# Modulation vectors of a two-block transformer kernel: column sums with TensorE replaced by row dot products on VectorE, with a new order of the opening and buffers moved to multiples of 512 bytes

## The reference: what is computed

```python
mod = silu(c) @ w_ada + b_ada            # 1024 -> 6 * 1024
sh1, sc1, g1, sh2, sc2, g2 = split(mod, 6)
h = rms_norm(x, norm_mix_g) * (1.0 + sc1) + sh1
proj = h @ w_in + b_in                   # 1024 -> 9224: GLU, q/k, v, o, gates, merge
a = glu; a = causal_depthwise_conv(a); a = silu(layer_norm(a)); y_conv = a @ w_conv_pw
y_mlstm = ...                            # chunkwise mLSTM over q, k, v and the gates
x = x + g1 * ((g_conv * y_conv + g_mlstm * y_mlstm) @ w_out)
h = rms_norm(x, norm_ffn_g) * (1.0 + sc2) + sh2
x = x + g2 * ((silu(h @ w_gate) * (h @ w_up)) @ w_down)
x = rms_norm(x, final_norm_g)
```

## Time and profile before

| | |
|---|---|
| median of 3 runs | 1706.56 us (1702.82 to 1707.67) |
| the profiled execution | 1704.14 us, of which the span in the trace is 1702.2 us |
| busy in the span | PE 1617.2 us, weight load 1312.4, DVE 1022.8, ACT 623.3, POOL 114.1 |
| mean granted TensorE clock | 0.977 of full speed |
| moved by DMA | 172.87 MB, 102 GB/s in the mean |

### The profile page before, as it was taken

The page is one execution under the profiler, slowest core; times in us unless marked ns, Lnnn a source line. Parts: engine busy times, 40 slices in busy tenths (PEclk is TensorE's granted clock), DMA queues, the critical chain, the costliest instruction groups (busy, mean ns, idle before and its releaser), DMA issues.

```text
span 1702.2 us, 18384 instructions
## 1 busy us (share of the span) xinstructions
PE 1617.2 (95%) x7176; PEld 1312.4 (77%) x7176; DVE 1022.8 (60%) x1527; ACT 623.3 (37%) x881; POOL 114.1 (7%) x94
## 2 busy tenths in 40 slices
PE   5999898999999899999999998999989999999988
PEld 4887776778778788888888886778867888888867
DVE  6699888889668644333464447766566444442255
ACT  3221465654442342222233233546453222222223
POOL 0000000000000000000011001000142111100010
PEclk9999988999899899999999999999999999999999
DMA  9133221222446334233332321211332333333332
GB/s 357 50 99 104 70 74 63 62 75 87 148 173 210 100 122 141 96 96 92 92 108 82 116 78 61 82 44 38 98 101 87 95 93 98 99 93 96 96 112 74
DMA packets 48191, 172.87 MB, mean 102 GB/s; under 512 B 5349, under 2 KB 5477, under 8 KB 47849
## 3 DMA queue, kind: packets, MB, share of 16 engines
q1 hardware_dynamic: 48104, 171.70, 31.6%
HBM read 167.48 MB, written 4.19 MB: 101 GB/s over the span
## 4 chain that ended last, share of the span: by engine, by line
PE 83%; DVE 11%; ACT 3%; issue 2%; DMA 0%; POOL 0%; SPq 0%; DVEq 0%; POOLq 0%; ACTq 0%
PE bank L1329 24%; PE bank L1330 24%; PE bank L1337 23%; DVE tmp L1874 1%; PE bank L1349 1%; DVE spl L1723 1%; PE bank L1351 1%; PE bank L1350 1%; DVE convout L1808 1%; PE bank L1432 1%; PE bank L1415 1%; PE bank L1445 1%; DVE XT L2211 1%; PE bank L1365 1%; ACT tmp L1498 1%
## 5 line engine op out<-in xcount | busy, mean ns | idle before, releaser
L1329 PE MATMUL bank<-HH,sph 128*128 128x512 f32 x1480 | 600.7, 406 | 28.9 <-DVE spl L1723 11.3
L1330 PE MATMUL bank<-HH,spl 128*128 128x512 f32 x1480 | 588.3, 397 | 0.0
L1723 DVE TENSOR_TENSOR spl<-raw,sph 128x1024 fp32r<-128x1024 f32 (+1 forms) x261 | 330.9, 1269 | 316.9 <-ACT sph L1490 316.5
L1337 PE MATMUL bank<-HL,sph 128*128 128x512 f32 x1480 | 385.9, 395 | 0.9 <-DVE HL L2215 0.9
L1329 PEld LDWEIGHTS bank<-HH,sph 128*128 128x128 f32 x1480 | 284.5, 192 | 100.6 <-issue 26.9
L1490 ACT ACTIVATE sph<-raw 128x1024 fp32r<-128x1024 f32 (+1 forms) x261 | 269.6, 1034 | 216.0 <-PE bank L1337 166.1
L1330 PEld LDWEIGHTS bank<-HH,spl 128*128 128x128 f32 x1480 | 285.0, 193 | 59.9 <-issue 1.4
L1337 PEld LDWEIGHTS bank<-HL,sph 128*128 128x128 f32 x1480 | 280.1, 190 | 63.2 <-DVE HL L2215 2.2
L1808 DVE SCALAR_TENSOR_TENSOR convout<-convin,vecs,convout 128x512 f32<-128x512 f32 x240 | 166.7, 745 | 0.0
L1329 PE MATMUL bank<-midh,sph 128*128 128x512 f32 x352 | 138.7, 394 | 0.0
L1330 PE MATMUL bank<-midh,spl 128*128 128x512 f32 x352 | 138.7, 394 | 0.0
(11 more groups left out here) (294 smaller groups left out, 1567.7 us busy)
## 6 DMA issues: line engine op xcount, KB each, us to landing
raw<-in_w_in SPq DMA_DIRECT2D x73, 512.0 KB, 3.6
raw<-in_w_up SPq DMA_DIRECT2D x66, 512.0 KB, 3.6
more<-in_w_ada SPq DMA_DIRECT2D x32, 512.0 KB, 4.5
raw<-in_w_down SPq DMA_DIRECT2D x32, 512.0 KB, 3.5
raw<-in_w_gate SPq DMA_DIRECT2D x22, 512.0 KB, 3.6
ada<-in_w_ada SPq DMA_DIRECT2D x16, 512.0 KB, 14.6
raw<-in_w_down SPq DMA_DIRECT2D x16, 384.0 KB, 3.1
raw<-in_w_v SPq DMA_DIRECT2D x8, 512.0 KB, 3.6
```

Source lines behind the costliest of these rows:

```text
L1329: e.matmul(P_[b][:], sph(n)[:, q], hi[:, k, :], start=k == 0, stop=False)
L1330: e.matmul(P_[b][:], spl(n)[:, q], hi[:, k, :], start=False, stop=False)
L1337: m = e.matmul(P_[b][:], sph(n)[:, q], low[:, k, :], start=False, stop=last and k == kb - 1)
L1723: e.tensor_tensor(spl(n), raw(n), sph(n).bitcast(F32), ALU.subtract).then_inc(*up("s_w_low", ("wl", n)))
```

## The change

Four parts.

1. `w_ada` is laid out transposed: one load of 512 KB now holds 128 outputs on the partitions and all 1024 inputs along them. A tile of `mod` is then one dot product on VectorE of the load with `silu(c)`, which stands as a row of 1024 on every partition (`crow`, a broadcast load, and a Silu of 128x1024 on ScalarE). Bias and sum are in the same instruction, and the products overwrite the load. `mod_sum`, `mod_far`, `mod_cols`, `mod_tiles` and `ada_columns` go, and with them all one-column matmuls of the modulation; `modacc` goes.
2. The opening's order: the loads begin with `x`, then the row of `c`, then `vecs` and `consts`; the Silu stands behind the squares of the first norm; the first four dot products stand ahead of the norm's root; from there each pair's dot products stand directly behind the low parts of the pair before, at k = 0 and 2 instead of at odd k.
3. The row of `c` is loaded and put through Silu a second time, after fence "gc", since its first place is used by others in between.
4. Buffers move: `base` from 16512 to 16896, `B` rounded up to a multiple of 512 bytes, `ah` and `al` too. So all high and low activations and the three weight slots start at multiples of 512 bytes. `sph_first`, `sph_second` and `spl_first` do not.

The first `csil` below is SyncE's, the second ScalarE's.

```diff
-    mod_a, mod_b, mod_c = misc.take(), misc.take(), misc.take()
...
-    csil, gmix = keepc(8), keepc(8)
-    add("csil", csil)
+    gmix = keepc(8)
     ss = SumSq("x0")
     for i in range(8):
         ss.add(("XT", i), [("x", 0, i)])
+    add("csil", 0)
+    add("mod_dots", 0)
     b0 = rows_of(ss, D)
...
     def mod_pair(p):
-        add("mod_far", p, mod_a[0], [("mod_half", p - 1)] if p else mod_a[1])
-        add("mod_cols", p, accs[p][0], mod_c[0], [("mod", p - 1)] if p else mod_c[1])
-        tmp.give(accs[p][0], ("mod_cols", p))
-        add("mod_tiles", p, mod_a[0], mod_c[0])
...
+        if p:
+            add("mod_dots", p)
+        low[p] = [tmp.take() for _ in range(2)]
         for z in range(2):
-            add("norm", "n1", 2 * p + z, *js[z], b0, [])
+            add("norm", "n1", 2 * p + z, *low[p][z], b0, [])
...
-    mod_sum(0, 0, 6)
     split()
     split()
     mod_pair(0)
-    mod_sum(1, 0, 3)
+    mod_low(0)
+    mod_pair(1)

     def mod_feed(k):
-        p = k // 2
-        if k % 2 == 0 and p < 3:
-            mod_sum(p + 1, 3, 6)
-            if p < 2:
-                mod_sum(p + 2, 0, 3)
-        if k % 2 and p < 3:
-            mod_pair(p + 1)
+        if k % 2 == 0 and k < 6:
+            mod_low(k // 2 + 1)
+            if k < 4:
+                mod_pair(k // 2 + 2)
+            else:
+                add("zero_pads")
...
     side.append(layer_norm())
+    add("csil", 1)
     add("ada_more", 0)
     add("ada_more", 1)
...
-        base = 16512
+        base = 16896
...
+        o += -(base + o) % 512
         B = o
+        CROW[0] = place("crow0", B + 13056, [128, 1024])
...
-        AH = place("ah", B + 33728, [128, 8, S], F32R)
-        AL = place("al", B + 33728 + 16384, [128, 8, S], F32R)
+        AH = place("ah", B + 33792, [128, 8, S], F32R)
+        AL = place("al", B + 33792 + 16384, [128, 8, S], F32R)
...
+            def csil(n):
+                if n:
+                    w.wait_ge(*fenced("gc"))
+                    e.dma_start(CROW[1][:], A["c_row"].broadcast_to([128, 1024])).then_inc(
+                        *up("d_c1", ("c_all", 1), by=16))
...
+            def csil(n):
+                w.wait_ge(at("c_all", n))
+                e.activation(CROW[n][:], CROW[n][:], ACT.Silu).then_inc(*up("s_ada_a", ("csil", n)))
...
+            def mod_dot(buf, n, et, label):
+                e.tensor_tensor_reduce(buf, buf, CROW[n][:], 1.0, vec("b_ada", et), ALU.mult, ALU.add,
+                                       MOD[:, et:et + 1]).then_inc(*up("s_ada", label))
+
+            def mod_dots(p):
+                w.wait_ge(at("csil", 0), at("vecs"))
+                for z in range(4):
+                    w.wait_ge(at("ada_w", p, z))
+                    mod_dot(ADA[4 * p + z][:], 0, 2 * p + z % 2 + 8 * (z // 2), ("mod", p, z))
...
             def ada(u):
-                k, s = u % 8, KEEP[:, u % 8:u % 8 + 1]
-                w.wait_ge(at("more", u))
-                if k == 0:
...
-                    ins = e.tensor_scalar(ACC[:], MORE[more(u)][:], s, None, ALU.mult)
-                else:
-                    w.wait_ge(at("ada", u - 1))
-                    ins = e.scalar_tensor_tensor(ACC[:], MORE[more(u)][:], s, ACC[:], ALU.mult, ALU.add)
-                ins.then_inc(*up("s_ada", ("ada", u)))
+                w.wait_ge(at("more", u), at("csil", 1))
+                mod_dot(MORE[more(u)][:], 1, 16 + u, ("ada", u))
```

More of the change, by code:

```diff
@@ L372, in plan, with mod_low @@
         ss.add(("XT", i), [("x", 0, i)])
+    add("csil", 0)
+    add("mod_dots", 0)
     b0 = rows_of(ss, D)
[L374 to L380, removed]
-    def mod_pair(p):
-        add("mod_far", p, mod_a[0], [("mod_half", p - 1)] if p else mod_a[1])
-        add("mod_cols", p, accs[p][0], mod_c[0], [("mod", p - 1)] if p else mod_c[1])
-        tmp.give(accs[p][0], ("mod_cols", p))
-        add("mod_tiles", p, mod_a[0], mod_c[0])
-        js = [tmp.take() for _ in range(2)]
+    low = {}
+    def mod_pair(p):
+        if p:
+            add("mod_dots", p)
+        low[p] = [tmp.take() for _ in range(2)]
         for z in range(2):
-            add("norm", "n1", 2 * p + z, *js[z], b0, [])
+            add("norm", "n1", 2 * p + z, *low[p][z], b0, [])
+    def mod_low(p):
         for z in range(2):
-            add("normlo", "n1", 2 * p + z, js[z][0])
-            tmp.give(js[z][0], ("hi", "n1", 2 * p + z), ("lo", "n1", 2 * p + z))
-    mod_sum(0, 0, 6)
+            add("normlo", "n1", 2 * p + z, low[p][z][0])
+            tmp.give(low[p][z][0], ("hi", "n1", 2 * p + z), ("lo", "n1", 2 * p + z))
     split()
@@ L1310, in end @@
                 w.wait_ge(at("out", 7))
-            run({"begin": begin, "load": load, "ada_load": ada_load, "ada_more": ada_more, "v_begin": v_begin, "rot_load": rot_load,
+            run({"begin": begin, "load": load, "ada_load": ada_load, "csil": csil, "ada_more": ada_more, "v_begin": v_begin, "rot_load": rot_load,
                  "w2_begin": w2_begin, "rd_load": rd_load, "p_load": p_load, "e_spill": e_spill,
@@ L1743, in spread @@
                         *up("s_scale", ("diag", name, t)))
[L1745 to L1770 removed]
+            def mod_dot(buf, n, et, label):
[6 more added lines that the diff above has]
+                    mod_dot(ADA[4 * p + z][:], 0, 2 * p + z % 2 + 8 * (z // 2), ("mod", p, z))
+                g8 = GMIX + 2 * p
+                w.wait_ge(at("mod", p, 3))
                 e.scalar_tensor_tensor(KEEP[:, g8:g8 + 2], MOD[:, 8 + 2 * p:10 + 2 * p], 1.0,
@@ L2321, in x2_lo @@
                         *up("s_cut_p", ("lo", "x2", i)))
-            run({"begin": begin, "split": split, "sum": total, "v_begin": v_begin, "decay_begin": decay_begin,
+            run({"begin": begin, "zero_pads": zero_pads, "split": split, "sum": total, "v_begin": v_begin, "decay_begin": decay_begin,
                  "normlo": normlo, "up": up_, "rope_full": rope_full, "mix_ret": mix_ret, "x2_lo": x2_lo,
@@ L2363, in layout @@
     o["pos"] = np.ascontiguousarray(x["positions_2"].reshape(1, S))
-    ada = x["w_ada"][0].reshape(8, 128, 6, 1024)
-    first = ada[:, :, 0:2].reshape(4, 2, 128, 2, 4, 256).transpose(4, 0, 2, 1, 3, 5)
-    o["w_ada1"] = np.ascontiguousarray(first).reshape(4, 4, 128, 2, 512)
-    o["w_ada2"] = np.ascontiguousarray(ada[:, :, 2:].transpose(2, 0, 1, 3)).reshape(32, 128, 1024)
+    ada = np.ascontiguousarray(x["w_ada"][0].T).reshape(48, 128, 1024)
+    pairs = [[2 * p + z % 2 + 8 * (z // 2) for z in range(4)] for p in range(4)]
+    o["w_ada1"] = np.ascontiguousarray(ada[np.array(pairs)])
+    o["w_ada2"] = np.ascontiguousarray(ada[16:])
+    o["c_row"] = np.ascontiguousarray(x["c"][0].reshape(1, D))
     o["w_in"] = _tiles(np.concatenate([win[:, 0:4096], win[:, 5120:6144], win[:, 6152:8200]], axis=1))
```

110 lines of the change are left out of this document (27 added, 83 removed).

## The result

| | before | after |
| --- | --- | --- |
| median of 4 runs each | 1704.69 us (1702.62 to 1707.67) | 1686.45 us (1686.18 to 1687.87) |
| profiled execution: time, span | 1704.14, 1702.2 us | 1687.87, 1686.1 us |

The ratio is 0.9893, with a 95% interval from 0.9874 to 0.9913: 18.2 us less. The forecast was 1686.6.

The account below looks back on a forecast made before the run. TensorE, busy 95% of the span, was taken as the bound, waiting for VectorE in the opening and behind fence "gc". Terms -6.8 - 6.8 + 2.6 - 8.9 = -19.9 us gave 1684.2, plus 2.4 for the median 1686.6; range 1677 to 1698.

Parts of the forecast that it names:

- Dot product at 1.3 us: Modulation on VectorE: one dot product over two SBUF tiles of 1024 costs 1.3 us, bounded by 1.15 and 1.5.
- half rate: Rival, chance 0.08: dot products run at half rate, 2.35 us each; time 1706 us, no change.
- The opening, 6.8 us saved: Opening: without column sums and the clock's fall, the last product of k = 8 starts at 61.5, not 68.33.
- So the early start is worth nothing: Opening: first product 1.3 us earlier, but the stall moves behind the third unit; k = 1 starts 0.4 us later.
- Second row of `c`, 2.6 us lost: Behind fence "gc": the second load and Silu delay the layer norm's chain, lengthening TensorE's wait; bounds 0 to 5 us.
- Column sums, 6.8 us saved: Later modulation: four column sums of 1.7 us each leave TensorE's queue; VectorE has room for 32 dot products.
- Addresses, 8.9 us saved: Matmuls: 1366 products each 6.5 ns faster once activation and weight start at the same place within 512 bytes.
- 352 bytes past: Placements before the change: the prediction put the starts of `midh` and `midl` 352 bytes past a multiple of 512.
- nothing: Rival, chance 0.10: the addresses give nothing, products stay at 233 ns; time 1695.5 us.
- frees the stream: Rival, chance 0.06: a multiple of 512 frees the stream altogether, 213 ns a product; time about 1603 us.
- collides: Rival, chance 0.05: two streams starting at multiples of 512 collide, 4728 `HH` products 6.5 ns longer; 1726 us.
- Sum: Whole kernel: the four terms total -19.9 us against the profiled 1704.14; with 2.4 for the median, 1686.6 us.

Follow-up runs that it names:

- splits first: Changed kernel with the splits of the third and fourth weight unit ahead of the second group of four dot products: 1683.48 us, ratio 0.9872.
- addresses only: Kernel before with only the change's addresses (base 16896, B at a multiple of 512, ah and al moved 64 bytes): 1698.88 us, ratio 0.9960.
- dots moved: Changed kernel with four of the eight dot products of the w_pw stage moved on into the w_out stage: 1680.13 us, ratio 0.9851.

## Why the prediction was right, point by point

- *Dot product at 1.3 us*: 1.21 from start to start, 1.28 in duration, and the short second instruction (84 ns) starts with the next one. Rival "half rate" is out.
- *The opening, 6.8 us saved*: 9.3. The mechanism was right: the third unit late (34.9; forecast 36.9), no column sums, no fall of the clock. VectorE's queue is the bound too, as "splits first" shows, though in the change itself the forecast wait of 0.4 us ahead of k = 6 did not come. The step that was mis-sized is the start: the row of `c` was ready at 12.6 and the weights at 13.5, not at 14.4, and with c = 1.21 thirteen dot products are 1.2 us shorter. The order of the loads alone is worth 2.2 to 3.3 us there. "So the early start is worth nothing" did not hold: k = 1 was to start at 39.0, 0.4 later than before, and started at 37.08, 1.5 earlier. What is worth nothing is only an earlier third unit, while VectorE's queue stays as long.
- *Second row of `c`, 2.6 us lost*: 3.5. The chain was the one named. The broadcast's result was there 4.5 us after its issue (420.98 to 425.48), not 3.9, and TensorE lost 0.7 more than the 2.8 by which L1551 was late.
- *Column sums, 6.8 us saved*: the step that failed in part. All four sums went, but in the stretch of the first three (5.1 us of the forecast, and 1.0 of the `ah` products) only 0.7 us were saved. The forecast said of VectorE's 32 dot products that it has room there. It hadn't: in the `w_pw` stage its rounds set the end already before ("addresses only"), the sum at 500.66 ran in their shadow, and a dot product in place of the cheaper L1783 (1.28 for 0.74) made one of them longer. TensorE, now faster, waited there for 2.9 us, and the half clock behind the second wait cost 1.7; "dots moved" gives both back. The remaining 1.7 us, of the longer window at 481.5, have no cause shown.
- *Addresses, 8.9 us saved*: the spacing came as forecast, at 227 ns everywhere; alone it was worth 6.8 us, as the `ah` products gained nothing in that same stage. The prediction's "352 bytes past" is a slip: by the placements `midh` and `midl` stood 320 past a multiple of 512, 192 from the weights. Rivals "nothing", "frees the stream" and "collides" are out.
- *Sum*: by spans 9.3 + 0.4 (up to the last gate, 429.06 against 419.41) - 3.5 + 0.7 + 9.3 = 16.2, where the spans differ by 16.1. The forecast of 19.9 was too large by 3.6 against the profiled execution: 2.9 too little up to the last gate, and too much by 0.9 for the row of `c`, by some 5.5 for the stage of `w_pw`. So the errors partly cancelled. That the median is met within 0.2 us is luck: the forecast took it 2.4 above the profiled execution, as before, and it lies 1.4 below, since this execution was the slowest of the four.

## What to carry to other kernels

Work taken out of TensorE's queue counts only where TensorE is the bound; look, stage by stage, at whether another engine's rounds are without idle time, even where TensorE never waits. A long wait is not always lost time, and moving its cause is worth nothing while another queue sets the end. Place the activations and the weights of a float32r matmul at equal offsets within 512 bytes: it was the fastest of the distances tried here.

## What the runs showed of the hardware

- A float32r product of 512 columns goes every 227 ns at full clock where both operands have the same offset within 512 bytes (0 or 128), every 230 ns at distances of 64 and 256 bytes, about every 232 at 128 (`ah` before), and every 233.3 ns at 192. Why 256 costs less than 192 stays open.
- A dot product over 1024 float32 from two SBUF tiles, with its sum, takes 1.28 us, as a pass of L1786 without one. The Trainium skill, "Vector Engine (DVE) Microarchitecture Reference", section "Points that are easy to get wrong", gives half throughput to the scalar-tensor-tensor shape with two such sources, for want of a read port for the accumulator. L1786 is of that shape and ran at 1.28; the dot product, another instruction, uses the accumulator and ran at 1.28 as well.
- Beside a POOL subtraction of the same size (2.74 us) it took 3.36 us.
